# Hybrid decoder step on one Trainium2 core: latents, retention and prompt attention as one stage with a written-out order

## What is computed

```python
h = rmsnorm(x, p['norm_w'])
z = h @ p['w_in']
q_r, k_r, v_r, g_r, q_lat, c_raw, kpe_raw, g_a = jnp.split(z, _split_points(), axis=-1)
q_r, k_r = rope(q_r), rope(k_r) * (RET_DK ** -0.5)
o_r, s_new = retention_scan(q_r, k_r, v_r, ret_s0, ret_chunk)
o_r = head_groupnorm(o_r, p['ret_gn_w']) * jax.nn.silu(g_r)
q = rmsnorm(q_lat, p['q_a_norm_w']) @ p['w_qb']
qn = rmsnorm(q[..., :MLA_NOPE], p['qn_w'])
qp = apply_rope(rmsnorm(q[..., MLA_NOPE:], p['qp_w']), cos_a, sin_a)
c = rmsnorm(c_raw, p['kv_a_norm_w'])
kpe = apply_rope(rmsnorm(kpe_raw, p['kp_w']), cos_a, sin_a)
o_a = attend(qn, qp, c, kpe, p) * jax.nn.silu(g_a)
y = x + jnp.concatenate([o_r, o_a], axis=-1) @ p['w_out']
```

## Time and profile before

| what | us |
|---|---|
| median of 3 runs (1431.44 to 1432.68) | 1431.53 |
| the profiled execution: its own time | 1431.1 |
| the profiled execution: its span | 1429.0 |
| layer 1: input projection | 0 to 194.0 |
| layer 1: latents | 194.0 to 264.4 |
| layer 1: retention and prompt attention | 264.4 to 351.5 |
| layer 1: cached attention | 351.5 to 649 |
| layer 1: output projection | 649 to 712 |
| layer 2: latents, retention and prompt attention | 905.0 to 1062.5 |

### The profile page before, as it was taken

How to read it: one execution, slowest core, us unless ns; L and a number is a source line. 1 busy time by engine, 2 the same in 40 slices (tenths; PEclk the granted TensorE clock), 3 DMA queues, 4 the chain that set the end, 5 groups by cost and what they waited for, 6 DMA issues and landing times.

```text
span 1429.0 us, 26883 instructions
## 1 busy us (share of the span) xinstructions
PE 1274.2 (89%) x8624; PEld 1158.3 (81%) x8624; DVE 733.0 (51%) x1392; ACT 532.0 (37%) x1382; POOL 422.9 (30%) x592
## 2 busy tenths in 40 slices
PE   5999988677999999978959999887879999999788
PEld 4999964456999999968959999545669999999688
DVE  4423256576466665554245233465765665566442
ACT  4312225232555555533042112252325555555330
POOL 1000143243444444430010001332435445444300
PEclk9999999698999999988979999996999999999899
DMA  9322030012352222202513120300123532222035
GB/s 309 134 94 94 0 80 1 1 31 72 96 180 75 76 79 79 77 7 91 182 65 126 63 94 0 80 1 1 31 74 94 181 84 79 77 74 75 1 109 178
DMA packets 132775, 115.85 MB, mean 81 GB/s; under 512 B 46514, under 2 KB 127347, under 8 KB 132659
## 3 DMA queue, kind: packets, MB, share of 16 engines
q1 hardware_dynamic: 132658, 114.52, 26.6%
HBM read 103.56 MB, written 13.27 MB: 82 GB/s over the span
## 4 chain that ended last, share of the span: by engine, by line
issue 50%; POOL 18%; PE 15%; POOLq 7%; DVE 5%; DVEq 2%; ACT 2%; DMA 0%; SPq 0%; ACTq 0%
POOL krs L1869 14%; POOL rstat L1758 3%; POOLq L1863 2%; POOLq L1865 2%; PE ps L540 2%; PE ps L541 2%; PE ps L542 2%; POOLq L1753 2%; PE ps L734 1%; DVEq L1547 1%; PE ps L721 1%; DVE mx L1548 1%; PE ps L883 1%; PE ps L912 1%; PE ps L549 1%
## 5 line engine op out<-in xcount | busy, mean ns | idle before, releaser
L1613 DVE TENSOR_REDUCE kss<-ksq 128x8 f32<-128x1024 f32 x128 | 156.0, 1219 | 217.0 <-ACT ksq L1222 217.0
L540 PE MATMUL ps<-w_hi,hT_hi 128*128 128x408 f32 (+2 forms) x704 | 244.2, 347 | 0.0
L541 PE MATMUL ps<-w_lo,hT_hi 128*128 128x408 f32 (+2 forms) x704 | 242.1, 344 | 0.0
L542 PE MATMUL ps<-w_hi,hT_lo 128*128 128x408 f32 (+2 forms) x704 | 241.3, 343 | 0.0
L1222 ACT ACTIVATE ksq<-ps 128x544 f32<-128x544 f32 x256 | 159.9, 624 | 200.1 <-PE ps L883 200.1
L883 PE MATMUL ps<-wq_hi,cT_hi 128*128 128x272 f32 x1024 | 223.7, 300 | 0.0
L1869 POOL TENSOR_TENSOR krs<-kss_t,cst 128x8 f32<-128x8 f32 x128 | 209.2, 1634 | 19.1 <-DVE Ssc L1627 2.5
L883 PE MATMUL ps<-wq_hi,cT_lo 128*128 128x272 f32 x1024 | 212.6, 289 | 0.0
L883 PE MATMUL ps<-wq_lo,cT_hi 128*128 128x272 f32 x1024 | 212.5, 289 | 0.0
L883 PEld LDWEIGHTS ps<-wq_lo,cT_hi 128*128 128x128 f32 x1024 | 161.9, 190 | 0.0
L883 PEld LDWEIGHTS ps<-wq_hi,cT_lo 128*128 128x128 f32 x1024 | 161.7, 190 | 0.0
(11 more groups left out here) (196 smaller groups left out, 2045.3 us busy)
## 6 DMA issues: line engine op xcount, KB each, us to landing
ckv<-in_cache_ckv SPq DMA_DIRECT2D x256, 128.0 KB, 2.0
raw<-in_w_in SPq DMA_DIRECT2D x68, 408.0 KB, 4.2
kp<-in_cache_kpe SPq DMA_DIRECT2D x256, 32.0 KB, 1.8
raw<-in_w_out SPq DMA_DIRECT2D x16, 340.0 KB, 4.2
S<-in_state_ret SPq DMA_DIRECT2D x8, 512.0 KB, 6.0
out<-S SPq DMA_DIRECT2D x8, 512.0 KB, 3.2
z<-out SPq DMA_DIRECT2D x2, 2048.0 KB, 7.9
wqb<-in_w_qb SPq DMA_DIRECT2D x3, 1152.0 KB, 9.0
```

Of the source, the lines that this page charges most:

```text
L540: pe.matmul(out, a_hi, b_hi, start=first, stop=False)
L541: pe.matmul(out, a_hi, b_lo, start=False, stop=False)
L542: return pe.matmul(out, a_lo, b_hi, start=False, stop=last)
L1613: dve.tensor_reduce(kss[:, hs, 2 * k:2 * k + 2, :], ksq[:, q % 2, :, c0:c0 + HW].rearrange("p j (h k) -> p j h k", h=H), AX.X, ALU.add).th ...
```

## The change

Stages 2 and 3 become one. `stage_end` is called with 2 where it was 3, and every engine has one written-out list of calls for the merged stage; the dependences are waits on semaphores as before.

- **Order.** Retention comes first (its sample tile right after the first projections), and each tile's latents, projections, turns and attention blocks follow one another mixed; the lists of the four engines were found by a search on a model of the engines.
- **PSUM.** Latents and projected queries share banks 0 and 1; values, keys, turned keys and turned rotary queries take turns in bank 2; scores *and* attended values of block n share bank 3 + n % 2, so `scores(n)` now waits for `attn_out(n - 2)`; turned queries and turned probabilities share bank 5; retention has banks 6 and 7. `cT`, `qnT`, `qpT`, `pr` and `prT` have two slots each.
- **Rotation of retention's q and k** moves into stage 1, in place in `z`, with unused columns of `z` as scratch; POOL's `rope_sin` and `decay_qk` move with it, and so do the retention gate (`gates_r`), the split of `w_kb` and the scaling of the query weight by SCALE. Groups 2 to 7 are written out in place of the loop.
- **Rotation of the rotary queries** moves from DVE to POOL (`rope_q`); DVE scales the rotary part in 4 products of 64 columns, before the other part.
- **Smaller:** the block maximum is negated by the reduction and its scaling instruction is gone; the sample tokens' own scores are scaled in 1 instruction, not 8; the copy `ks` is gone.
- **SP** issues all of sequence 0's pages after `absorb`; sequence 1's follow after the merged stage.

```diff
     NBLK = H * S_TILE
-    STEPS = (2, 5, 8, 11, 14, NBLK + 1)
+    TURN_AFTER = (-1, 1, 4, 8, 11)
...
             sp.wait_ge(out_done, 16 * OUTS)
-            sp.wait_ge(kvs_ps, 3)
-            load_seq(0, 0, None, range(0, 2))
+            sp.wait_ge(absorb_ps, 1)
+            load_seq(0, 0, None)
...
             def scores(n):
                 i, h = divmod(n, H)
+                if h == 0:
+                    pe.wait_ge(q_kept, i + 1)
+                    pe.wait_ge(qp_kept, i + 1)
+                    pe.wait_ge(k_kept, i + 1)
                 if n >= 2:
-                    pe.wait_ge(p_ok, n - 1)
+
+                    pe.wait_ge(po_ok, n - 1)
...
+            scores(5)
+            attend(4)
+            q_turn(2)
+            q_project(3)
+            turn_probs(5)
...
+            keep_z(2)
+            split(4, 0)
+            rope_tiles(0, 1)
+            keep_z(3)
+            split(5, 1)
+            rope_tiles(2, 3)
+            keep_z(4)
...
+            def rope_cos(t):
...
+                dve.tensor_tensor(rope_t(t)[0].rearrange("p h a k -> p (h a) k"), src,
+                                  tab.to_broadcast((n, 4 * H, DK // 2)), ALU.mult)
...
+            rope_sin(0)
+            rope_sin(1)
+            for t in range(TILES):
+                decay_qk(t)
+                if t + 2 < TILES:
+                    rope_sin(t + 2)
...
+            def rope_q(t):
...
+                for k, name in enumerate(("cos_a", "sin_a")):
+                    tab = const_view(name)[0:n, t * half:(t + 1) * half].rearrange("p (o k) -> p o k", o=1)
+                    pool.tensor_tensor(qp[0:n, 1 + k, :, :].rearrange("p h (a k) -> p (h a) k", a=2), q0,
+                                       tab.to_broadcast((n, 2 * H, half)), ALU.mult)
...
-                dve.tensor_reduce(mx[:, n, 0:1], ps[:, 4 + n % 2, 0:(i + 1) * P], AX.X, ALU.max)
-                dve.drain()
-                dve.tensor_scalar(mx[:, n, 1:2], mx[:, n, 0:1], -SCALE, None, ALU.mult).then_inc(sc_max, 1)
+                dve.tensor_reduce(mx[:, n, 1:2], ps[:, 3 + n % 2, 0:(i + 1) * P], AX.X, ALU.max, negate=True)\
+                    .then_inc(sc_max, 1)
```

More of the change, by code:

```diff
@@ new lines, in absorb @@
+            def absorb():
+                pe.wait_ge(q_kept, TILES)
+                pe.wait_ge(qp_kept, TILES)
+                pe.wait_ge(wkbT_kept, 1)
+                for c in range(KC):
+                    for h in range(H):
+                        n = c * H + h
+                        m = pe.matmul(ps[:, 2, n * ST:(n + 1) * ST], wkbT[:, h, c * P:(c + 1) * P],
+                                      qnT[:, S_TILE % 2, h, 0:ST], start=True, stop=True)
+                m.then_inc(absorb_ps, 1)
@@ new lines, in _ @@
+            scores(1)
+            step_update(1)
+            k_project(1)
+            turn_probs(0)
+            step_update(2)
+            turn_probs(1)
+            attend(0)
+            latents(2)
+            q_turn(1)
+            attend(1)
+            step_update(3)
+            scores(2)
+            q_project(2)
+            k_turn(1)
+            ret_turn(1)
+            scores(3)
+            turn_probs(2)
+            qp_turn(1)
+            ret_scores(1)
+            attend(2)
@@ new lines, in _ @@
+            v_project(2)
+            turn_probs(3)
+            scores(4)
+            ret_out(1)
+            attend(3)
+            k_project(2)
+            turn_probs(4)
+            latents(3)
+            scores(5)
[3 more added lines that the diff above has]
+            turn_probs(5)
+            scores(6)
+            k_turn(2)
+            ret_turn(2)
+            attend(5)
+            qp_turn(2)
+            ret_scores(2)
+            scores(7)
+            turn_probs(6)
@@ new lines, in _ @@
+            v_project(3)
+            ret_out(2)
+            attend(6)
+            k_project(3)
+            turn_probs(7)
+            latents(S_TILE)
+            scores(8)
+            attend(7)
+            q_project(S_TILE)
+            turn_probs(8)
+            scores(9)
+            ret_turn(3)
+            attend(8)
+            q_turn(3)
+            k_turn(3)
+            ret_scores(3)
+            scores(10)
+            turn_probs(9)
+            ret_out(3)
+            attend(9)
@@ new lines, in _ @@
+            qp_turn(3)
+            turn_probs(10)
+            scores(11)
+            attend(10)
+            k_project(S_TILE)
+            scores(12)
+            turn_probs(11)
+            ret_turn(S_TILE)
+            attend(11)
+            q_turn(S_TILE)
+            qp_turn(S_TILE)
+            scores(13)
+            turn_probs(12)
+            absorb()
+            ret_scores(S_TILE)
+            turn_probs(13)
+            attend(12)
+            ret_out(S_TILE)
+            scores(14)
@@ L848, in _ @@
+            attend(13)
+            new_scores()
+            scores(15)
+            turn_probs(14)
+            attend(14)
+            turn_probs(15)
+            attend(15)
+            stage_end(pe, 1)
             CUT = (HQ + HW) // 2
```

1005 lines of the change are left out of this document (587 added, 418 removed).

## The result

| | before | changed |
|---|---|---|
| median, us (lowest to highest) | 1432.11 (1431.44 to 1433.44), 4 runs | 1339.80 (1336.52 to 1342.53), 4 runs |
| ratio, 95% interval | | 0.9353 (0.9330 to 0.9377) |
| profiled execution: time, span, us | 1431.1, 1429.0 | 1340.8, 1338.9 |

What follows compares the result with a forecast made beforehand. PE was taken to bound the kernel. In the merged stage 112 us of PE's work plus 17 idle make 129 against 157.5, saving 28.5 a layer: 1431.1 - 57 = 1374 us, range 1348 to 1406.

Steps and rivals of the forecast that it cites:

- PE's work, packed: In the merged stage, PE's busy time of 122.2 us falls to 112 us; the ends are 105 and 122.
- PE's idle time: In the merged stage, PE's waits sum to 17 us a layer, against 35.3 before.
- start: At the merged stage's start PE waits 3 us for the first tile's latents to be turned and copied.
- middle: In the merged stage's middle, scores wait for the output of block n - 2; PE idles 7 us.
- end: At the merged stage's end blocks 14 and 15 stand alone, and PE idles 4 us.
- input projection, SP's pages, `S0`: Work moved into the input projection, later page loads and `S0` cost 0; uncovered, up to 6, 6 and 2 us.
- the 10 us: In the merged stage, a denser PE list has less half-clock time, taking 10 us off PE's 122.2 busy.
- The other reference: Cached attention, also a written list of mixed chains, idles 6%, which on 120 us is 7 to 8.
- DVE's load doesn't matter: In the merged stage DVE falls from 100.3 to about 80 us, isn't the bound, and its saving is not added.
- The hold behind POOL: In the input projection POOL's products block DVE's on SBUF: 2.60 us instead of 1.22; rival 1380, chance 0.02.
- Long round trips: Rival: in the merged stage eight block pairs at 15.4 us make it 146 us, time 1408; chance 0.22.
- the denser case: Rival: in the merged stage PE's work 108 and idle 10 make 118 us, time 1352; chance 0.10.

## Why the prediction came out 34 us too high

The terms of the sum beside what the profile shows, per layer:

| term | forecast | measured |
|---|---|---|
| merged stage | 129 | 113.8, 112.8 |
| PE's work, packed | 112 | 111.0, 109.5 |
| PE's idle time: start | 3 | 0, 0.4 |
| middle | 7 | 0.8, 0.7 |
| end | 4 | 1.4, 1.4 |
| meeting | 3 | 0.7, 0.7 (and 2.2 ahead of the stage) |
| DVE, POOL busy | 80, 49 | 71.2, 48.2 |
| input projection, SP's pages, `S0` | 0 | 0.5 less in layer 1; no wait for them |

- **Where time can be won: right.** The gain lies in the merged stage alone, and PE bounds before and after.
- **PE's work, packed: right.** 112 against 111.0 and 109.5. The clock in the stage went from 0.89 and 0.87 to 0.99 and 1.00, as the 10 us assumed. PE's busy time fell by 11.2 and 15.3. The old order with its waits filled shows what holding the clock is worth without the new order: 14 us for both layers, 7 each. The Trainium skill (TensorE: Matmul & The Clock Gate, What's actually happening) has activity release the throttle; by that rule the 112 stays, and the trace agrees, with 1.00 in the dense stage.
- **PE's idle time: wrong, and this is the step that failed.** 17 was forecast, 2.9 and 3.2 measured. Two layers of 14 make 28 of the 31 us by which the stages came out shorter than 129, PE's work the other 3.5. Of the 34 us, 2.4 more come from the stage before, which I took as 157.5 in both layers; to cached attention's first product it had 157.8 and 159.6. Of the pieces, "In the middle the bank rule counts ... I take 7" was the worst. I compared 6 us of PE's work between a block and the next but one with a round trip of 7.5 plus queueing, taken from rows of the old order. The exponent done twice shows the slack. The two extra tanh at the start are covered by the turn of `wkb`, but for 0.4 us in layer 2 (with all five tanh ahead of the copies, as in the run with ACT's list changed, PE waits 4.3), and the last two blocks fill each other's waits: two of 0.69 are left.
- **The other reference was wrong too.** Cached attention's 6% of idle is no floor for a written list. This stage idles 2.5 and 2.9%.
- **DVE's load doesn't matter: wrong as I put it.** DVE isn't the bound at 64% or 63%, but what the relief is worth is not nothing: 11 to 12 us a layer in the old order, and 12 for half of DVE's part in the new. DVE's queue stands in the chains. With the work put back PE idles 10.6 and 13.4 us in the stage instead of 2.9 and 3.2, so 8 to 10 of the 14 us of idle time that I had too much hang on this term. And DVE's busy time was 9 under my 80.
- **Input projection: right.** The stretch 92 to 134 is full (42.00 of 42.00), with DVE at 26.7 instead of 13.6 and POOL at 16.2 instead of 0. The hold behind POOL came as feared, and stayed hidden. In the row that I had read for it, DVE's product ended 1.08 us after POOL's, not 1.22. DVE's mix at 96.98 takes 2.39 us where the one before takes 0.68. It begins behind POOL's product and ends 0.55 after it:

```profile
95.78 0.68 DVE L1527 TENSOR_TENSOR z<-z 128x512 f32<-128x512 f32 x1
...
96.54 2.28 POOL L2032 TENSOR_TENSOR z<-z,cst 128x1024 f32<-128x1024 f32 x1 [17.84 <-DVE z L1527]
96.98 2.39 DVE L1527 TENSOR_TENSOR z<-z 128x512 f32<-128x512 f32 x1
```

- **The rivals.** Long round trips (1408) had 0.22 and the denser case (1352) 0.10; what came was denser than that one. For a searched list the weight belonged the other way round: the searched order is made to shorten the very trips that I took from the old one (14.1 to 9.5).

Not settled: how much of the 60 us belongs to merging the two stages, how much to the new banks and how much to the search, since the old order, which turns all tiles' queries before the first block, can't be written with two slots for turned queries. Nor was POOL's list changed alone.

## What to carry to other kernels

When a written order is changed, the waits and round trips of the old one are no measure of the new. For a list that a search has packed, take PE's packed work as the floor, and add idle time only where the list has nothing else to give, as at its ends; for a plain list that would be far off (89 us of idle time here). Where a step goes through another engine, put short steps of other chains between its halves, and look at what stands in front of it in the other engine's list. Check every engine's list for this, since naive lists on the followers cost more (53 us a layer) than the whole change gained (45). An engine at 64% still costs time if its steps stand in the chains of the bound one: price it by putting the work back.

## What the runs showed that I had not expected

- Idle time is paid twice. In the plain order 89 us of gaps came with a clock of 0.70, and the same 656 products were busy 171 us instead of 111.
- Short gaps were followed by the low clock too. At the layer boundary 23.9 us at 0.50 begin inside PE's gap of 13.9 and last 14 us beyond it, with further gaps in them (9.0 us busy in all). With one meeting in the middle, a single gap of 2.9 us was followed by 3.4 us at 0.50; in the changed kernel the gap of 2.2 ahead of the merged stage was too in layer 1 (194.4 to 197.8) and not in layer 2.
- Useless products in PE's waits paid for themselves in the old order: 111 more a layer, and 7 us a layer less. In the changed kernel 153 a layer took 8 us off, and 80 more gained nothing further.
